# SwiGLU gate and up products turned round: weight tiles stationary, 256 tokens moving

## The reference, cut to what matters

```python
def swiglu(h, w_g, w_u, w_d):
    return (jax.nn.silu(h @ w_g) * (h @ w_u)) @ w_d
...
hx2 = modulate(rms_norm(x_mixed, g_ffn[l]), sh2, sc2)
x = x_mixed + gt2 * swiglu(hx2, w_ffn_gate[l], w_ffn_up[l], w_ffn_down[l])
```

## Time and profile before

| | |
|---|---|
| time, three runs | 1657.17, 1658.67, 1658.84 us; median 1658.67 us |
| profiled execution | 1656.88 us, span 1655.2 us |
| PE busy | 1614.1 us, 98% of the span, 7915 matmuls |
| DVE busy | 1100.5 us, 66% |
| ACT busy | 729.8 us, 44% |
| POOL busy | 158.7 us, 10% |
| data moved | 389.13 MB, mean 235 GB/s |
| mean granted TensorE clock | 0.993 |

### The profile page before, as it was taken

The page is one execution under the profiler, slowest core; times in us unless marked ns, Lnnn a source line. Parts: engine busy times, 40 slices in busy tenths (PEclk is TensorE's granted clock), DMA queues, the critical chain, the costliest instruction groups (busy, mean ns, idle before and its releaser), DMA issues.

```text
span 1655.2 us, 22919 instructions
## 1 busy us (share of the span) xinstructions
PE 1614.1 (98%) x7915; PEld 1325.8 (80%) x7915; DVE 1100.5 (66%) x1261; ACT 729.8 (44%) x813; POOL 158.7 (10%) x294
## 2 busy tenths in 40 slices
PE   5999999999999999999999999999999999999998
PEld 3667888987788888888877888888888888888876
DVE  4233545879788788878877566767765556456577
ACT  5333233557744444444445543443434434434334
POOL 1002011000012212122010001101100000000000
PEclk9999999999999999999999999999999999999999
DMA  9998547555479989899676568778776666666653
GB/s 341 357 355 244 192 139 224 179 165 165 148 253 330 325 273 324 275 336 341 235 251 209 153 222 262 261 232 280 240 267 190 190 191 189 190 191 189 190 166 139
DMA packets 200249, 389.13 MB, mean 235 GB/s; under 512 B 14368, under 2 KB 47376, under 8 KB 199296
## 3 DMA queue, kind: packets, MB, share of 16 engines
q1 hardware_dynamic: 177168, 312.63, 58.5%
q0 software_dynamic: 23024, 75.74, 13.4%
HBM read 385.30 MB, written 3.01 MB: 235 GB/s over the span
## 4 chain that ended last, share of the span: by engine, by line
PE 86%; DVE 5%; DMA 4%; ACT 3%; issue 1%; SPq 1%; DVEq 0%; ACTq 0%
PE ps L1367 24%; PE ps L1369 23%; PE ps L1368 23%; PE ps L1339 4%; PE ps L1341 4%; PE ps L1340 4%; DMA BR<-in_w_mod 3%; DVE LO L767 2%; PE ps L1335 2%; DMA RAW<-in_w_in 1%; ACT HI L439 1%; PE ps L1421 1%; PE ps L1528 0%; PE ps L1515 0%; SPq L282 0%
## 5 line engine op out<-in xcount | busy, mean ns | idle before, releaser
L767 DVE TENSOR_TENSOR LO<-RAW,HI 128x1024 fp32r<-128x1024 f32 x520 | 633.9, 1223 | 426.2 <-ACT HI L439 424.9
L439 ACT ACTIVATE HI<-RAW 128x1024 fp32r<-128x1024 f32 x520 | 549.2, 1060 | 782.4 <-PE ps L1369 663.2
L1367 PE MATMUL ps<-HI,H 128*128 128x512 f32 x1856 | 728.6, 393 | 3.6 <-DVE LO L767 3.0
L1369 PE MATMUL ps<-HI,H 128*128 128x512 f32 x1856 | 722.7, 389 | 0.0
L1368 PE MATMUL ps<-LO,H 128*128 128x512 f32 x1856 | 722.3, 389 | 0.0
L1367 PEld LDWEIGHTS ps<-HI,H 128*128 128x128 f32 x1856 | 348.4, 188 | 79.8 <-DVE LO L767 4.1
L1369 PEld LDWEIGHTS ps<-HI,H 128*128 128x128 f32 x1856 | 348.3, 188 | 73.1
L1368 PEld LDWEIGHTS ps<-LO,H 128*128 128x128 f32 x1856 | 348.5, 188 | 72.7 <-issue 1.7
L409 POOL DMA_DIRECT2D BR<-in_w_mod x224 | 120.5, 538 | 770.2 <-DVE BR L866 318.9
L866 DVE SCALAR_TENSOR_TENSOR BR<-BR,SCF 128x512 f32<-128x512 f32 (+1 forms) x210 | 156.7, 746 | 20.5 <-DMA BR<-in_w_mod 19.7
L1339 PE MATMUL ps<-H,HI 128*128 128x256 f32 (+1 forms) x384 | 126.7, 330 | 0.1
(11 more groups left out here) (252 smaller groups left out, 771.8 us busy)
## 6 DMA issues: line engine op xcount, KB each, us to landing
RAW<-in_w_gate SPq DMA_DIRECT2D x128, 512.0 KB, 4.7
BR<-in_w_mod POOLq DMA_DIRECT2D x224, 256.0 KB, 4.7
RAW<-in_w_ffn_gate SPq DMA_DIRECT2D x88, 512.0 KB, 3.8
RAW<-in_w_ffn_up SPq DMA_DIRECT2D x88, 512.0 KB, 3.8
RAW<-in_w_ffn_down SPq DMA_DIRECT2D x88, 512.0 KB, 3.6
RAW<-in_w_in SPq DMA_DIRECT2D x64, 512.0 KB, 4.8
BR<-in_w_mod SPq DMA_DIRECT2D x50, 512.0 KB, 9.4
RAW<-in_w_branch SPq DMA_DIRECT2D x32, 512.0 KB, 5.6
```

Source lines behind the costliest of these rows:

```text
L439: act.activation(HI[:, j % RING, :], RAW[:, j % RING, :], ACT.Copy).then_inc(hi_done, 1)
L767: tt(LO[:, j % RING, :], RAW[:, j % RING, :], HI[:, j % RING, :], ALU.subtract).then_inc(lo_done, 1)
L1367: mm(o, xh, wh, start=first and t == 0, stop=False, skip_group_check=True)
L1369: i = mm(o, xl, wh, start=False, stop=last and t == 1, skip_group_check=True)
```

## The change

From the second chunk on, gate and up products are made by `piece` in place of `piece_rows`. The hidden activations then come out with features on the partitions, HD already has the layout that the down products want, and `hidden_turn` is left out except for chunk 0, whose products are made as before. ACT and DVE read HD in SBUF where they read banks 2 and 3, and ACT waits for `hid_float`, raised by `hidden`, where it waited for `hid_turned`, raised by the transposes. Because chunk 1 still turns chunk 0, it is written out ahead of the loop on PE, ACT and DVE, and the loop runs over chunks 2 to 9.

```diff
             def hidden_high(m, hid=HID):
-                act.wait_ge(s("hid_turned"), m + 1)
-                act.activation(hid[:, :, 0, :], pair(2).rearrange("p b (k t) -> p (b k) t", k=2), ACT.Copy).then_inc(s("hid_hi"), 1)
+                if isinstance(m, int) and m == 0:
+                    act.wait_ge(s("hid_turned"), 1)
+                    src = pair(2).rearrange("p b (k t) -> p (b k) t", k=2)
+                else:
+                    act.wait_ge(s("hid_float"), m + 1)
+                    src = HD.rearrange("p (k t) -> p k t", t=T)
+                act.activation(hid[:, :, 0, :], src, ACT.Copy).then_inc(s("hid_hi"), 1)
...
             def hidden_low(m, hid=HID):
                 dve.wait_ge(s("hid_hi"), m + 1)
-                tt(hid[:, :, 1, :], pair(2).rearrange("p b (k t) -> p (b k) t", k=2), hid[:, :, 0, :], ALU.subtract)\
+                if isinstance(m, int) and m == 0:
+                    src = pair(2).rearrange("p b (k t) -> p (b k) t", k=2)
+                else:
+                    src = HD.rearrange("p (k t) -> p k t", t=T)
+                tt(hid[:, :, 1, :], src, hid[:, :, 0, :], ALU.subtract)\
                     .then_inc(s("hid_lo"), 1)
...
             def gate_pieces(m, base):
                 pe.wait_ge(s("ffn_gate_read"), m)
                 for j in range(8):
-                    piece_rows(base + j, j, tokens_of(HX), row_banks(0), 2 * j, j == 0, j == 7)
-                    if j == 1:
-                        hidden_turn(m - 1)
+                    piece(base + j, j, only_x, halves(0), 2 * j, j == 0, j == 7)
+                    if j == 1 and isinstance(m, int) and m == 1:
+                        hidden_turn(0)
 
             def up_pieces(m, base):
-                pe.wait_ge(s("hid_lo"), m)
+                if isinstance(m, int) and m == 1:
+                    pe.wait_ge(s("hid_lo"), 1)
+                else:
+                    pe.wait_ge(s("hid_float"), m)
                 for j in range(8):
-                    piece_rows(base + j, j, tokens_of(HX), row_banks(2), 2 * j, j == 0, j == 7)
-
-            with pe.Fori(1, FC - 1) as m:
+                    piece(base + j, j, only_x, halves(2), 2 * j, j == 0, j == 7)
+
+            def ffn_chunk(m):
                 base = LOOP0 - 24 + m * 24
                 gate_pieces(m, base)
...
+
+            ffn_chunk(1)
+            with pe.Fori(2, FC - 1) as m:
+                ffn_chunk(m)
             gate_pieces(FC - 1, PRE0)
...
                 down_group(PRE0 + 16 + 2 * i, i, n, HIDL if m == FC - 1 else HID, m == FC - 2, m == FC - 1)
-                if i == 0:
-                    hidden_turn(FC - 1)
```

More of the change, by code:

```diff
@@ L723, in _, with chunk @@
                     ffn_gate(0, FFN0 + 7)
-            with act.Fori(1, FC - 1) as m:
+            def chunk(m):
                 base = LOOP0 - 24 + m * 24
@@ L731, in _ @@
                         ffn_gate(m, base + 7)
+            chunk(1)
+            with act.Fori(2, FC - 1) as m:
+                chunk(m)
             for w in range(32):
@@ L1237, in chunk @@
                     if mod and w >= 8:
-                        mod_tile(m + 11, w - 8, ACCG[:, bass.ds(m - 1, 1), :].rearrange("p o n -> p (o n)"))
+                        mod_tile(m + 11, w - 8, ACCG[:, m - 1, :] if isinstance(m, int) else ACCG[:, bass.ds(m - 1, 1), :].rearrange("p o n -> p (o n)"))
                     if w == 3:
@@ L1247, in chunk @@
                         down(m - 1, n, base + 9 + 2 * n)
-            with dve.Fori(1, 5) as m:
+            chunk(1, True)
+            with dve.Fori(2, 5) as m:
                 chunk(m, True)
```

## The result

The changed kernel takes 1675.1 us (four runs, 1674.55 to 1675.93) against 1657.92 before (four runs, 1657.11 to 1658.84). The ratio is 1.0104, with an interval of 1.0092 to 1.0116: slower by 1.0%. The forecast was 1675.2 us, 16.5 above a median of 1658.67 for the kernel before; with a fourth run that median is 1657.92, and the measured difference is 17.2.

What follows compares the result with a forecast made beforehand. The prediction took PE to bound the feed-forward part, with ACT and DVE waiting for it. Its terms, 25.3 - 9.05 + 0.3 = +16.5 us on a median of 1658.67, gave 1675.2 us, with an 8-in-10 range of 1670.5 to 1681.5.

Steps and rivals of the forecast that it cites:

- Term 1: Gate and up pieces of chunks 1 to 10: 24 matmuls of 256 columns replace 12 of 512, +25.3 us.
- term 3: Each of ten chunks passes once from `piece` to `piece_rows`, with slightly slower steps behind it: +0.3 us.
- Term 2: Ten of the eleven turns of eight transposes on PE are left out, 0.905 us each: -9.05 us.
- Term 4: Moved waits, such as ACT's `hidden_high` waiting for DVE's `hidden` and no longer for PE: no cost.
- Halves cost half: Rival: in the feed-forward part two 256-column matmuls take no longer than one of 512; 1649.6 us, faster; chance 0.04.
- The sequencer becomes the limit: Rival: PE's register operations and loop branches are no longer hidden, 5.8 us more, 1681.0 us; chance 0.08.

Runs made afterwards that it cites:

- The costing part alone: The changed kernel with all eleven turns of transposes kept, the later results unread: 1683.17 us, ratio 1.0159 to the kernel before.
- the other operand stationary: Kernel before without the ten turns, tokens stationary, each gate and up matmul of 512 columns made as two of 256: 1674.74 us, ratio 1.0107.
- the cut at 320: Kernel before without the ten turns, tokens stationary, each gate and up matmul of 512 columns split 320 + 192: 1708.42 us, ratio 1.0305.
- 576 matmuls: Kernel before without the ten turns, only gate pieces split to 128 columns, up left at 512: 1861.0 us.
- the run with 864 matmuls in the loop: Kernel before without the ten turns, gate and up matmuls split to 128 columns: 2376.71 us, ratio 1.4344.
- the run with 960: The changed kernel with two chunks in each turn of PE's loop, same work: 1686.85 us, ratio 1.0182 to the kernel before.

## Why the prediction was right

**What bounds the part.** PE, as read: the changed kernel has no wait of PE of more than 1.4 us in the table, and the time follows PE's matmuls and, in the long loops, its branch.

**Term 1, +25.3 us.** The distance in the loop is 0.120 us, and a chunk grew as foretold, to 67.86 against 67.8. ACT's releases in gate and up are 2.88 us apart, so the term measures 160 x 0.160 = 25.6. The costing part alone, with term 3 in it, measured 26.0. At the full clock the remainder of 0.0133 us per matmul held with the other operand stationary and with the cut at 320, so it is a cost per matmul and not of this form. What makes it is open.

**Term 2, -9.05 us.** Measured alone as 9.8 by the medians and 0.91 a chunk by the trace. Eight transposes in 0.88 us are 0.11 each, near the 0.1117 us of narrow matmuls; that the cause is the same is likely, and no run isolates it.

**Term 3, +0.3 us.** ACT's releases show it: the first down piece of a chunk stands 2.74 us behind the last gate piece, from 1323.89 to 1326.63 us, and the others 2.72 apart. That is 0.02 each, 0.2 in all. With it the terms as measured give 25.6 - 9.1 + 0.2 = 16.7 us, and the stretch shows 16.66.

**Term 4, nothing.** ACT's rounding of the last chunk waited 0.45 us for DVE's `hidden` behind its `high`, at 1626.11, where the earlier trace rows shows 2.47 of waiting; as foretold nobody was waiting for it.

**Luck.** That 1675.1 us lies 0.1 from the forecast is in part luck: the start was 0.75 us too high and the difference 0.7 too low. What the traces bear out is the 16.5 us, within 0.2.

**Rivals.** *Halves cost half* fell in the loop itself. The Trainium skill's formula on the page "TensorE: Matmul & The Clock Gate", section "Back-to-back issue gap", which would have made the change faster, does not hold for this stream of loads and matmuls, and the prediction did not say that the page gives it for an isolated matmul, beside other figures for streams with loads. At the full clock the measured distance is columns / 2.4 + 13 ns, with a floor of 112 ns, where the page's formula has 2.5 ns. *The sequencer becomes the limit* fell as well: in the changed kernel no longer step stands at piece borders though each has its 32 ns operation. But a relative of it was nearer than I had thought. I counted the loop's branch at its 0.215 us and did not ask whether the instructions of a longer loop are still held by PE when it turns. By the branch's row it does not wait at 480 and at 576 matmuls, and it does at 864. Had the change taken in two chunks a turn, its forecast would have missed by 12 us.

## What to carry to other kernels

Where PE bounds, price a change of its matmuls by start-to-start distances of the same widths in the trace, never by busy time or by columns alone: here, at the full clock and with a stationary tile of 128 columns loaded for each, a matmul costs its columns and 13 ns, and below some 236 columns, by an estimate from these runs (0.1117 less 0.0133, times 2.4 GHz), a floor of 112 ns takes over. Trading wide matmuls for a layout that needs no transposes pays only if the contraction is short: a chunk pays 192 x 0.0133 = 2.6 us for 0.9 us of turns at 16 row tiles of contraction, so by an estimate from these rows the two meet at five or six tiles. And before making the body of a hardware loop longer, compare the instruction packets in the page and the duration of the loop's branch: where the packets rose with the turns here and the branch took over 4 us in place of 0.215, each turn cost a gap and in most cases a slow stretch.

## What the runs showed of the hardware that was not expected

At the lower clock the 13 ns are gone, and 128 and 256 columns cost the same. The first two rows are matmuls of 512 columns in the run with 864 matmuls in the loop, the next two matmuls of 256 in the run with 960, each at a granted clock of 0.50:

```profile
1260.59 0.63 PE L1383 MATMUL ps<-HI,H 128*128 128x512 f32 x1
1261.01 0.63 PE L1381 MATMUL ps<-HI,H 128*128 128x512 f32 x1
```

```profile
1306.88 0.41 PE L1355 MATMUL ps<-H,LO 128*128 128x256 f32 x1
1307.10 0.41 PE L1353 MATMUL ps<-H,HI 128*128 128x256 f32 x1
```

Over more steps (1260.59 to 1263.15 and 1306.46 to 1309.66) the distances are 0.427 us for 512 columns and 0.213 for 256, which is the columns at 1.2 GHz and nothing more. For 128 columns it is 10.24 / 48 = 0.2133, which is 256 cycles of 1.2 GHz. At the full clock the floor of 0.1117 us is 268 cycles of 2.4 GHz. So in this number format 256 columns are about where floor and columns meet, at either level.

That the load of the stationary tile makes the floor is likely, though no run leaves a load out. Two rows of PEld's timeline in the kernel before speak for it: the loads of 128 columns for four matmuls that move only 4 columns each, at a clock of 1.00, and behind them loads of 32 columns:

```profile
33.10 0.52 PEld L1434 LDWEIGHTS ps<-BR 128*128 128x128 f32 x4 [0.97 <-ACT BR L485]
35.85 0.23 PEld L1421 LDWEIGHTS ps<-BR 128*32 128x32 f32 x8 [2.22 <-issue]
```

With 0.19 us for one load, the four stand (0.52 - 0.19) / 3 = 0.11 us apart, as those of matmuls with 128 columns do, so the floor does not hang on the columns that move. Eight loads of 32 columns fit in 0.23 us, so it is not the pace at which loads can be issued either.

The two long loops turn ten times, each with a gap of 2.2 to 3.1 us. In nine cases the granted clock was 0.50 less than 1 us behind the gap, after matmuls at full pace ahead of it. With 256-column matmuls behind it the clock was back at 1.00 within 5 us of the gap's end; with 128-column matmuls it stayed at 0.50 for more than 80 us, though PE was busy without a break, and came back only when 512-column matmuls ran. The Trainium skill's page "Runtime: NRT & Kernel Launch", section "Instruction fetch mechanics", says that a taken branch to a target that is no longer held makes the engine wait for a fetch. The runs agree, and price it here: 2.5 us a turn where the clock stays up, 4.2 to 4.4 where it falls before 256-column matmuls, and 44 where it falls before 128-column ones. That PE waits for the branch is read from its rows; that the branch waits for a fetch rests on the packets and on the loop lengths, since the fetch itself has no row. Between 576 and 864 matmuls no run tells where the limit lies. The tenth case, the first turn of the loop with 960 matmuls, has the shortest gap, 2.21 us, and the clock stayed up; why is open.
